# Attention slots of a two-layer hybrid transformer: value products moved to odd slots, the first index search moved behind the first scaling

## What is computed

```python
o_mla = _dense_causal_attention(q, k, kv[..., MLA_NOPE:], (MLA_NOPE + MLA_ROPE) ** -0.5, None)
o_fox = _dense_causal_attention(f_q, f_k, f_v, HEAD_DIM ** -0.5, jnp.cumsum(log_f, axis=1))
o_dsa = _dsa_attention(s_q, s_k, s_v, i_q, i_k, i_w, positions, slopes, topk)
proj = jnp.einsum('bsnc,ncd->bsnd', branches, w_branch)
merged = jnp.einsum('bsnd,bsnd->bsd', gates, proj)      # then merged @ w_out
```

## Time and profile before

| | |
|---|---|
| median of 3 runs | 850.48 us (850.42 to 851.19) |
| the profiled execution's own time | 850.96 us |
| its span, first to last instruction | 849.2 us |
| PE busy | 834.6 us, 98% |
| DVE busy | 606.1 us, 71% |
| ACT busy | 463.7 us, 55% |
| POOL busy | 106.0 us, 12% |
| granted TensorE clock, mean | 0.997 |

### The profile page before, as it was taken

One profiled execution on the slowest core, in us unless ns is written; L12 is line 12 of the kernel. 1 busy time (PEld: TensorE's weight loads), 2 busy tenths in 40 slices (PEclk: granted clock), 3 DMA queues, 4 the chain that ended last, 5 costly groups with the idle time before them and its releaser, 6 DMA issues.

```text
span 849.2 us, 15725 instructions
## 1 busy us (share of the span) xinstructions
PE 834.6 (98%) x6332; PEld 777.8 (92%) x6332; DVE 606.1 (71%) x1084; ACT 463.7 (55%) x707; POOL 106.0 (12%) x131
## 2 busy tenths in 40 slices
PE   8999999999999999999999999999999999999996
PEld 7899899999899999988889998998998999999885
DVE  5675787887886877765676558788877787777554
ACT  5655777673356655543446476676535465555430
POOL 1502800005400000000000066000071000000000
PEclk9999999999999999999999999999999999999998
DMA  9859643435578677475836693434456777764731
GB/s 306 233 129 273 190 138 101 136 120 183 159 199 222 189 193 193 160 239 179 268 111 182 144 324 103 145 104 150 134 165 194 193 208 198 196 188 150 240 121 49
DMA packets 180856, 150.98 MB, mean 178 GB/s; under 512 B 22348, under 2 KB 154032, under 8 KB 180528
## 3 DMA queue, kind: packets, MB, share of 16 engines
q1 hardware_dynamic: 171712, 143.08, 57.1%
q10 hardware_dynamic: 9072, 6.90, 2.9%
HBM read 148.63 MB, written 1.06 MB: 176 GB/s over the span
## 4 chain that ended last, share of the span: by engine, by line
PE 89%; DVE 3%; DMA 3%; POOLq 2%; POOL 1%; issue 1%; ACT 0%; DVEq 0%; ACTq 0%; SPq 0%
PE ps L651 27%; PE ps L653 27%; PE ps L652 27%; PE ps L925 2%; DMA decay<-decay_rows 2%; PE ps L956 2%; POOLq L1948 2%; PE ps L937 2%; PE ps L709 1%; POOL rel_first L1945 1%; DVE w_lo L1455 1%; DVE prob L1611 1%; POOL decay_first L1934 1%; PE ps L904 0%; PE ps L905 0%
## 5 line engine op out<-in xcount | busy, mean ns | idle before, releaser
L1455 DVE TENSOR_TENSOR w_lo<-raw,w_hi 128x2048 fp32r<-128x2048 f32 (+3 forms) x142 | 304.6, 2147 | 110.9 <-ACT w_hi L1118 110.8
L651 PE MATMUL ps<-xt_hi,w_hi 128*128 128x256 f32 x1232 | 345.6, 281 | 0.0
L652 PE MATMUL ps<-xt_lo,w_hi 128*128 128x256 f32 x1232 | 341.1, 277 | 0.0
L653 PE MATMUL ps<-xt_hi,w_lo 128*128 128x256 f32 x1232 | 341.0, 277 | 0.0
L1118 ACT ACTIVATE w_hi<-raw 128x2048 fp32r<-128x2048 f32 (+3 forms) x142 | 252.6, 1784 | 83.2 <-PE ps L653 75.7
L651 PEld LDWEIGHTS ps<-xt_hi,w_hi 128*128 128x128 f32 x1232 | 231.6, 188 | 3.4 <-issue 2.4
L652 PEld LDWEIGHTS ps<-xt_lo,w_hi 128*128 128x128 f32 x1232 | 231.6, 188 | 0.1
L653 PEld LDWEIGHTS ps<-xt_hi,w_lo 128*128 128x128 f32 x1232 | 231.5, 188 | 0.0
L651 PE MATMUL ps<-w_hi,ht_hi 128*128 128x512 f32 x176 | 68.6, 390 | 0.0
L652 PE MATMUL ps<-w_lo,ht_hi 128*128 128x512 f32 x176 | 68.5, 389 | 0.0
L653 PE MATMUL ps<-w_hi,ht_lo 128*128 128x512 f32 x176 | 68.5, 389 | 0.0
(11 more groups left out here) (231 smaller groups left out, 1277.7 us busy)
## 6 DMA issues: line engine op xcount, KB each, us to landing
raw<-ffn_w_up SPq DMA_DIRECT2D x88, 512.0 KB, 5.2
raw<-w_in SPq DMA_DIRECT2D x84, 512.0 KB, 6.2
raw<-ffn_w_down SPq DMA_DIRECT2D x32, 512.0 KB, 4.2
raw<-w_branch SPq DMA_DIRECT2D x24, 512.0 KB, 4.4
raw<-w_out SPq DMA_DIRECT2D x16, 512.0 KB, 4.4
raw<-ffn_w_down SPq DMA_DIRECT2D x24, 256.0 KB, 2.9
decay<-decay_rows ACTq DMA_DIRECT2D x2, 1024.0 KB, 9.3
ln_g<-ln_g ACTq DMA_DIRECT2D x4, 512.0 KB, 3.6
```

Source lines behind the costliest of these rows:

```text
L651: pe.matmul(dst, a_hi, b_hi, start=first, stop=False)
L652: pe.matmul(dst, a_hi, b_lo, start=False, stop=False)
L653: return pe.matmul(dst, a_lo, b_hi, start=False, stop=last)
L1455: ins = dve.tensor_tensor(panel_lo(l, p)[0:n, cols], panel_raw(l, p)[0:n, cols], panel_hi(l, p)[0:n, cols].bitcast(F32), ALU.subtract)
```

## The change

`values` of groups 0 to 4 go to slots 7, 11, 15, 19 and 23, in front of the scores of that slot; group 5 stays in slot 26. `outputs_hi` and `outputs_lo` of these groups go one slot on, to 8, 12, 16, 20 and 24. Round 0 of the index search goes from the end of slot 2 to slot 3, behind `normalise` of pair 0 and in front of round 1. No instruction is added or taken away.

```diff
-        def fourth_slot_pairs(s, lag):
-
-            return [i // 2 for i in even_slot_pair(s, lag) if i % 2]
+        def values_in(s):
+
+            return {LAST_SLOT: [PAIRS // 2 - 1]}.get(s, [(s - 7) // 4] if s % 4 == 3 and 7 <= s < SLOTS else [])
...
                     if SLOTS <= s:
                         branch_panel(l, s - SLOTS, (0, 1))
+                    for g in values_in(s):
+                        values(l, g)
                     for i in even_slot_pair(s, LAG_S):
                         scores(l, i)
                     for i in even_slot_pair(s, LAG_T):
                         turn_probs(l, i)
-                    for g in fourth_slot_pairs(s, LAG_V):
-                        values(l, g)
...
                     for i in even_slot_pair(s, LAG_E):
                         softmax_exp(l, i, 0)
                         softmax_exp(l, i, 1)
-                    for g in fourth_slot_pairs(s, LAG_V + 1):
+                    for g in values_in(s - 1):
                         outputs_hi(l, g)
...
                     for i in even_slot_pair(s, LAG_E + 1):
                         if i < PAIRS - 1:
                             normalise(l, i)
-                    for g in fourth_slot_pairs(s, LAG_V + 1):
+                    for g in values_in(s - 1):
                         outputs_lo(l, g)
                     if s == SLOTS:
                         merge(l, 0, (0, 1))
...
-                    if 2 <= s < 18:
+                    if s == 3:
+                        take_eight(l, 0)
+                    if 3 <= s < 18:
                         take_eight(l, s - 2)
```

## The result

| | before | changed |
|---|---|---|
| median of 20 runs | 850.48 us (849.1 to 851.19) | 851.98 us (851.68 to 853.18) |
| span of the profiled execution | 849.2 us | 850.0 us |
| PE busy | 834.6 us | 834.5 us |
| mean granted TensorE clock | 0.997 | 0.998 |

The ratio is 1.0025, with a 95% interval of 1.0019 to 1.0031: slower by 1.5 us in the medians and by about 2 us in the ratio, where no change was forecast. The range, 847.0 to 852.6, holds it; the loss was missed.

A forecast was written before the change was run, and what follows sets the result against it. PE was taken as the bound, busy for 834.6 of 849.2 us, so time could come only from its work or few waits. Terms 3.0 + 2.1 - 0.6 - 4.5 = 0.0 gave a median of 850.4 us, range 847.0 to 852.6.

The forecast's parts named there:

- part 2: Values in front of scores in odd slots: 1.07 us saved per layer, 2.1 us gain in all, bounds 0 and 3.1.
- Part 1: Index search round 0 behind the scaling in slot 3: waits shrink, 3.0 us gain, bounds 1.0 and 3.6.
- Rival B: Scaling beside POOL holds up POOL's index scores by 1.66 us; part 1 shrinks by 2.2 us: 852.6 us, chance 0.07.
- Part 3: outputs_lo in slot 20, in front of pair 9's scaling: second half of transposes late, 0.6 us loss, bounds 0 and 1.
- Part 4: outputs_lo in slot 24 waits for outputs_hi and delays the merges: 2.26 us a layer, 4.5 us loss, bounds 3 and 5.
- The first range: The forecast's own range for the kernel's time, said to come from the parts' bounds: 848.8 to 852.1 us.
- Rival C: Switch from values to scores costs a full round trip, 1.75 us inserted; part 2 is 0: 852.5 us, chance 0.11.

The follow-up runs named there:

- e1: Kernel before with only round 0 of the index search moved behind the first scaling, values left in even slots: 847.77 us, ratio 0.9967 to the kernel before.
- e3: Changed kernel with group 4's values alone back in slot 22 and its copies in slot 23: 848.38 us, ratio 0.9979.
- e4: Changed kernel with only outputs_lo of group 4 moved from the front of slot 24 to the end of VectorE's slot 25: 848.38 us, ratio 0.9977.
- e10: Changed kernel with outputs_hi of group 4 in front of ScalarE's exponentials in slot 24 instead of behind them: 848.74 us, ratio 0.9987.
- e5: e4 with values between scores and transposes instead of in front of scores: 846.78 us, ratio 0.9961.
- e7: e1 with four idle transposes of the identity behind values in slots 6, 18 and 22: 849.71 us, one run.

## Why the prediction was wrong

The step that failed is part 2: it was put at a gain of 2.1 us and brought a loss of about 0.1. The other three terms were right in kind.

- **Part 1, right in kind, a little small.** Forecast 3.0 us; the traces give 1.50 (10.10 - 8.60) in the first layer and 1.91 (10.71 - 8.80) in the second, 3.4 together, and e1's stretch 3.4. The rest of the wait in slot 5, put at 0.3 us a layer, did not come: the split in slot 4 took 2.29 us, where it took 2.79 before, so DVE's chain was shorter than the 7.16 us that the forecast carried over. The split of the kernel before:

```profile
100.05 2.79 DVE L1455 TENSOR_TENSOR w_lo<-raw,w_hi 128x2048 fp32r<-128x2048 f32 x1
```

- **Rival B fell.** Scaling beside POOL took 1.22 us, and the index scores came only 0.25 us after DVE asked for them in the first layer and 0.90 in the second. The rule of the Trainium skill ("SBUF — State Buffer", Who interferes with whom) is about one instruction and not about a row of them; the trace shows POOL's addition beside the scaling at 0.57 us (at 93.49) against 0.46 undisturbed (at 90.22). That is the 0.1 us that part 1 took for it, and POOL did not stand still for the whole scaling.
- **Part 2, the step that failed.** Forecast: 1.50 us inserted in front of scores, 1.07 us saved per layer. The insertion was right where the tiles around it are short-spaced: slots 22 and 23 take 8.57 us, with 8.62 forecast. But the sum charged a visit to its own pair of slots alone and booked "a slower gate tile after it" as something that goes away with the switch. It did not go away: in the odd slot the long spacing lasts over two tiles and more, until a later group ends it. So the four pairs without a visit, which the sum left alone, lost 0.2 us each, 0.8 per layer, and slots 18 and 19 saved 0.11 instead of 0.25. For MLA's groups the saving was nothing (9.97 and 9.97, 9.54 and 9.53, where 0.16 was forecast): scores took 1.41 us behind values instead of 1.31, and 0.09 us more stand between head transposes and values than between head transposes and scores. The gain of 0.72 and the loss of 0.78 leave a loss of 0.06 us per layer, 0.1 for both. Of the 445 additional long-spaced matmuls about 310 stand in these slots, 1.4 us; most of the others are in slots 24 to 26, where PE waits for merges anyway. The rows priced the visit, and no row priced its after-effect in another place; the bound of 0 nearly held it.
- **Part 3, too large**: forecast 0.6 us, measured 0.2. The scaling of slot 21 starts 0.24 us behind PE's scores (171.44 against 171.20), where it started 0.17 us ahead of them before (172.85 against the second line here):

```profile
171.44 1.01 DVE L1611 TENSOR_SCALAR prob<-prob,rinv 128x128 f32<-128x128 f32 x4
```

```profile
173.02 0.93 PE L925 MATMUL ps<-sk_t,sq_t 64*128 64x128 f32 x8
```

It came 0.41 us later against PE and not 0.61, and the difference is what the long-spaced tiles of slots 20 and 21 held PE itself up, 0.20. So part 3 came out small through what part 2 had missed.
- **Part 4, right**: forecast 2.26 us a layer; from branch tile 0 to tile 7 the trace gives 12.60 us (193.97 - 181.37) against 10.39 (193.77 - 183.38), so 2.21. e3, e4 and e10 take it away and part it.
- **The sum**: 3.4 - 0.1 - 0.2 - 4.4 is a loss of 1.3 us, where the stretches give 1.4 and the medians 1.5. That the forecast missed by no more is partly luck: parts 1 and 3 came out 0.8 us better than forecast and hid as much of the 2.2 us that part 2 lacked. The first range, 848.8 to 852.1, is narrower than the bounds that it is said to come from: the low ends of parts 1 and 2 alone take away 2.0 and 2.1 us.
- **Rival C** had the number (852.5) and the value of part 2 (0) by another way: it made the insertion dear, 1.75 us, and the visit took 1.45. The rule on changes of tiling mode ("TensorEngine Tiling (Array Packing)", Key Properties, of the Trainium skill) spoke for the low end, and the saving did come out low, but no run shows that a drain did it: the visit takes 1.45 us in front of scores as in front of a gate tile, and what was lost stands in tiles further on.

**What stays open**: what sets and what ends the long spacing. It follows values in most places, ends behind the MLA groups of slots 9 and 13, and ended at each of PE's waits for merges of 0.3 us and more in the changed kernel. But the same scores and transposes end it in slot 19 of the kernel before and not in slot 17 of the changed one; in the changed kernel the tiles of slots 4 and 5 are short-spaced in one layer and long-spaced in the other, with the same groups in front of them; and the tile of slot 8 is short-spaced behind values in the second layer of e4 and e5. None of the runs separates the causes further.

## What to carry to other kernels

When a copy moves to a neighbouring slot, read what stands in front of it there on both of its engines: the same two instructions cost nothing in slots 8 to 16 and 2.2 us in slot 24, where the split that used to cover ACT's work was missing. When two independent edits come in one change, run each alone: one was worth 3 us and the other cost more. And a price taken from rows for "one visit" holds for the visit and not for the slots behind it; when PE is busy throughout, compare the same slots before and after, those that nothing was moved into as well, down to the spacing of their matmuls.

## What was not expected of the hardware

The clock is not it: the windows of slots 6 to 23 show a granted clock of 1.00 in both kernels. The columns are us, then busy us (and instructions) of PE, its weight loads, DVE, ACT and POOL, the granted clock, the DMA share and GB/s; before, then changed:

```profile
106.00:183.00 77.00, 77.00 (x668) 70.98 (x667) 62.40 (x192) 51.83 (x121) 1.31 (x3) 1.00 0.38 122
```

```profile
106.00:183.00 77.00, 76.99 (x667) 71.30 (x666) 61.07 (x186) 50.76 (x117) 2.82 (x2) 1.00 0.39 127
```

In both, identical fp32r matmuls of 256 columns run 113.3 or 117.8 ns apart, for tiles on end. The same tile has either spacing in different kernels, and moving or adding groups in front of it changes it (e5, e7); slots 4 and 5 show that these groups alone do not fix it. The changed kernel has 445 more matmuls at the long spacing, at 4.5 ns each 2.0 us of 850, as much as the change itself moved; the part of it in slots 24 to 26 is hidden under waits.
